# Level, state and convolution updates of VectorE in an earlier place, and two more unread products at the start

## The reference

```python
# block 1
mod = silu(c) @ ada_w + ada_b                     # 1024 x 6144, six vectors of 1024
h = rmsnorm(x, norm_mix_w) * (1 + sc1) + sh1
proj = h @ w_in                                   # 1024 x 3624, split into eleven parts
o_a = hgrn2_mixer(...)    # decayed linear recurrence, 4 heads of 128
o_b = dsa_mixer(...)      # scores, 128 best keys of each query, softmax, 4 heads of 64
o_c = conv_module(...)    # gate, causal depthwise convolution of 31 taps, layer norm
x = x + g1 * (concat(o_a, o_b, o_c) @ w_out)
x = x + g2 * (square(relu(h2 @ mlp_w1)) @ mlp_w2) # 4096 hidden channels
# block 2, layer A: gMLP mixer with 2048 channels
# block 2, layer B: RG-LRU, 12 heads of 128
xc = conv_b + sum over k of conv_w[k] * xb[t - 3 + k]     # 4 taps
r, i = sigmoid(xc @ gate_a_w + b), sigmoid(xc @ gate_x_w + b)
h[t] = a[t] * h[t-1] + sqrt(1 - a[t]**2) * i[t] * xc[t]   # a from r
x = x + (h * silu(g)) @ w_out
```

## Time and profile before

| | |
|---|---|
| median of 3 runs | 1294.99 us (1294.63, 1294.99, 1299.47) |
| the profiled execution | 1300.01 us |
| its span, first to last instruction | 1298.4 us |
| TensorE busy | 1258.8 us, 97% of the span |
| VectorE busy | 850.4 us, 66% |
| ScalarE busy | 584.2 us, 45% |
| mean granted clock of TensorE | 0.989 |

### The profile page before, as it was taken

One profiled execution on the slowest core, in us unless ns is written; L12 is line 12 of the kernel. 1 busy time (PEld: TensorE's weight loads), 2 busy tenths in 40 slices (PEclk: granted clock), 3 DMA queues, 4 the chain that ended last, 5 costly groups with the idle time before them and its releaser, 6 DMA issues.

```text
span 1298.4 us, 18826 instructions
## 1 busy us (share of the span) xinstructions
PE 1258.8 (97%) x6611; PEld 1024.2 (79%) x6611; DVE 850.4 (66%) x1275; ACT 584.2 (45%) x840; POOL 108.0 (8%) x149
## 2 busy tenths in 40 slices
PE   4999999999999999999999999999999999999997
PEld 3777778688788888888888888888888887777786
DVE  5889987648675322444444887775476668977863
ACT  4575545432354211333332665333233347878732
POOL 9124210000000000000000000110010000000000
PEclk9899999989999999999999999999999999999999
DMA  9677852315536333333332223324232241332131
GB/s 344 181 204 155 180 124 82 114 49 169 172 115 191 99 97 97 94 98 99 96 93 87 82 65 98 98 88 123 82 93 85 82 122 57 100 107 78 56 97 65
DMA packets 209084, 146.63 MB, mean 113 GB/s; under 512 B 7490, under 2 KB 191985, under 8 KB 209024
## 3 DMA queue, kind: packets, MB, share of 16 engines
q1 hardware_dynamic: 200672, 134.40, 34.4%
q0 software_dynamic: 6128, 10.38, 4.4%
q10 hardware_dynamic: 2224, 1.05, 0.3%
HBM read 135.06 MB, written 2.10 MB: 106 GB/s over the span
## 4 chain that ended last, share of the span: by engine, by line
PE 75%; DVE 13%; ACT 5%; issue 5%; DMA 2%; POOL 1%; DVEq 0%; ACTq 0%; POOLq 0%; SPq 0%
PE banks L404 23%; PE banks L406 22%; PE banks L405 22%; ACT w_hi L376 2%; DVE w_lo L388 1%; DVE xc L2438 1%; DMA cT<-in_c 1%; PE banks L708 1%; POOL e L2647 1%; DVE vh L2338 1%; DVE hgt L1900 1%; DVE acc_sh L1805 1%; DMA hq<-in_ada_w 1%; PE banks L1143 1%; PE banks L1088 1%
## 5 line engine op out<-in xcount | busy, mean ns | idle before, releaser
L388 DVE TENSOR_TENSOR w_lo<-raw,w_hi 128x1024 fp32r<-128x1024 f32 x204 | 250.8, 1234 | 127.2 <-ACT w_hi L376 122.2
L404 PE MATMUL banks<-h_hi,w_hi 128*128 128x512 f32 x792 | 319.8, 404 | 1.1 <-issue 0.5
L406 PE MATMUL banks<-h_hi,w_lo 128*128 128x512 f32 x792 | 310.4, 392 | 0.0
L405 PE MATMUL banks<-h_lo,w_hi 128*128 128x512 f32 x792 | 310.4, 392 | 0.0
L376 ACT ACTIVATE w_hi<-raw 128x1024 fp32r<-128x1024 f32 x204 | 213.4, 1051 | 156.2 <-PE banks L406 137.6
L404 PEld LDWEIGHTS banks<-h_hi,w_hi 128*128 128x128 f32 x792 | 150.1, 190 | 41.1 <-issue 9.2
L405 PEld LDWEIGHTS banks<-h_lo,w_hi 128*128 128x128 f32 x792 | 150.2, 190 | 33.7 <-issue 3.8
L406 PEld LDWEIGHTS banks<-h_hi,w_lo 128*128 128x128 f32 x792 | 149.9, 189 | 32.0
L404 PE MATMUL banks<-n_hi,w_hi 128*128 128x512 f32 x288 | 113.5, 394 | 0.9 <-DVE e L2400 0.9
L406 PE MATMUL banks<-n_hi,w_lo 128*128 128x512 f32 x288 | 112.1, 389 | 0.0
L405 PE MATMUL banks<-n_lo,w_hi 128*128 128x512 f32 x288 | 112.1, 389 | 0.0
(11 more groups left out here) (398 smaller groups left out, 1864.4 us busy)
## 6 DMA issues: line engine op xcount, KB each, us to landing
raw<-in_mlp_w SPq DMA_DIRECT2D x64, 512.0 KB, 3.8
raw<-in_a_w_in SPq DMA_DIRECT2D x48, 512.0 KB, 3.8
raw<-in_w_in SPq DMA_DIRECT2D x28, 512.0 KB, 4.2
raw<-in_ada_w SPq DMA_DIRECT2D x26, 512.0 KB, 4.2
raw<-in_b_w_in SPq DMA_DIRECT2D x24, 512.0 KB, 3.7
raw<-in_a_w_out SPq DMA_DIRECT2D x16, 512.0 KB, 3.4
raw<-in_b_w_out SPq DMA_DIRECT2D x16, 384.0 KB, 3.0
raw<-in_w_out SPq DMA_DIRECT2D x8, 512.0 KB, 4.0
```

Source lines behind the costliest of these rows:

```text
L388: dve.tensor_tensor(dst, src, hi, ALU.subtract).then_inc(split_lo, 1)
L404: pe.matmul(dst, l_hi, r_hi, start=first, stop=False)
L405: pe.matmul(dst, l_hi, r_lo, start=False, stop=False)
L406: return pe.matmul(dst, l_lo, r_hi, start=False, stop=last)
```

## The change

TensorE waits at the start after two more tiles (14 and 15) and runs `keep_busy()` after each, seven products for five. On VectorE, `level(6)` runs ahead of `lo_unit(25)` instead of behind it. `state(1)` stands at the end of slot 26 instead of in the middle of slot 27, and `state(2)` at the end of slot 27 instead of in slot 28. In the RG-LRU layer `conv(1, 2)` stands in turn 1 ahead of `recurrence(1, 1)`, with `lo_unit` of unit 12 in front of it, instead of at the start of turn 2; for that turn 2 is written out, and the loop is left with turns 3 and 4. ScalarE, GpSimd and SyncE keep their order.

```diff
-            for n in range(KT + 1, 2 * KT - 2):
+            for n in range(KT + 1, 2 * KT):
                 pe.wait_ge(ada_dve, n)
                 keep_busy()
...
             def slot(u):
 
+                level_first = u == U_LEVEL + 7
+                if level_first:
+                    level(u - U_LEVEL - 1)
                 lo_unit(dve, u + LEAD)
...
-                if U_LEVEL < u <= U_LEVEL + N_LEVELS:
+                if U_LEVEL < u <= U_LEVEL + N_LEVELS and not level_first:
                     level(u - U_LEVEL - 1)
...
                 if u == U_ATT + 4:
                     gate(1)
-                    state(1)
                     conv_scaled()
                 if u == U_ATT + 5:
                     gate(2)
                     softmax_in(3)
-                    state(2)
...
                 if u == U_ATT + 3:
                     softmax_out(2)
+                    state(1)
+                if u == U_ATT + 4:
+                    state(2)
...
-                if not first and more != "second":
+                if not first and more not in ("second", "third"):
                     conv(1, i)
...
                 recurrence(0, i)
-                if more is True and not first:
+                if more and more != "second" and not first:
                     conv(0, i + 1)
-                if first:
+                if first or more == "second":
                     lo_unit(dve, U_B + 5 + LEAD, i)
+                if more == "second":
+                    conv(1, i + 1)
                 recurrence(1, i)
-                if more and not first:
+                if more and more != "second" and not first:
                     lo_unit(dve, U_B + 5 + LEAD, i)
...
             turn(1, False, "second")
-            with dve.Fori(2, B_HEADS // 2 - 1) as i:
+            turn(2, False, "third")
+            with dve.Fori(3, B_HEADS // 2 - 1) as i:
                 turn(i, False, True)
```

## The result

The changed kernel takes 1288.91 us on the median of 8 runs (1286.99 to 1290.83), the kernel before 1297.12 us on the median of 8 beside it (1294.48 to 1301.30). The medians lie 8.2 us apart, 0.6%. The recorded ratio of the runs, which isn't the quotient of these two medians, is 0.9928, 95% interval 0.9911 to 0.9945: 0.7% faster. The profiled execution took 1288.7 us with a span of 1287.1, so 11.3 us of span are gone against the profile of before.

What follows compares the result with a forecast made beforehand. TensorE, busy 1258.8 of 1298.4 us, was taken as the bound, so only its pauses and half clock could be won. Terms 1.6 + 4.8 + 3.2 + 0.3 gave 9.9 us, 8.7 for the median: 1286 us, range 1281.5 to 1291.5.

Steps and rivals of the forecast that it cites:

- my sum: Gains of slot 22, states, conv and start added: 9.9 us for the profiled execution, 8.7 us for the median's.
- my signs of being right: No wait at three places, full clock behind, new pauses of about 1.6 and 1.0 us, `turn_probs(3)` 7 to 8 us sooner.
- my signs of being wrong: Half clock at 202 to 206 us, column sums after 34.7 us, pause above 2 us before turn 3, unexplained VectorE wait.
- Slot 22: `level(6)` moved ahead: 2.4 us gained with a new 1.6 us pause, 1.6 us after half a possible fall.
- States: `state(1)` and `state(2)` earlier in slots 26 to 28: 4.8 us gained, 2.8 without the clock's fall, 3.8 for the median.
- The conv of turn 2: `conv(1, 2)` earlier in the RG-LRU layer: 3.2 us gained, 1.8 without the fall, new pause of 1.0 us.
- The start: Two more products ahead of the column sums: net gain 0.3 us, bounds -1.9 and 2.9.
- push the column sums back by some 0.2 us: At the start, two more products delay the column sums by some 0.2 us, up to 1.9 at half clock.
- Rival 1: At all places, clock plays no part and only pauses are won: 7.0 us, 1288.0 us; chance 0.10.
- Rival 2: At slot 22, start and turn 3, new pauses replace the old: 2.5 us gained, 1292.5 us; chance 0.17.
- rival 3: Across the places, more falls go than counted: 12.9 us gained, 1282.1 us; chance 0.10.
- 4: Rival 4: turn 2's new straight code on VectorE waits for instructions, up to 15.7 us, giving 1302 us; chance 0.03.

Runs made afterwards that it cites:

- the first experiment: The kernel before with only the two more unread products at the start: 1296.93 us on the median of 12 runs, ratio 0.9985.
- the second profile of before: The kernel before, unchanged, profiled once more: one execution of 1296.08 us.
- the seventh: The changed kernel with `join(1)` right behind `level(6)` in slot 22: 1289.32 us on the median of 6, ratio 0.9928.
- the eighth experiment: The changed kernel with `yb_high(1, 1)` behind `read_gates(1, 2)` and `yb_low(1, 1)` behind VectorE's second input product: 1287.37 us, ratio 0.9910.
- the last two kernels: The changed kernel with `join(1)` forward, `yb_high(1, 1)` later and column sums halved: 1286.62 us with seven products at the start, 1284.68 us with five.

## Why the prediction was right

Predicted were 1286.0 us, 9.0 us below the median of before as it then stood, which is 0.7%; measured was 0.7% by the ratio and 8.2 us by the medians, for the 8.7 of my sum. The time itself came out 2.9 us higher. Most of that is the reference: beside the changed kernel, and in 59 later runs, the kernel before took 1293.96 to 1302.43 us with medians of 1297.1, 1299.2, 1299.0 and 1300.0, and the three runs of 1294.99 us were good ones. That the median's executions are some 5 us shorter than the profiled one was wrong: the profiled 1300.01 us lies 0 to 3 us above these four medians.

For the profiled execution I had 9.9 us, to 1290.1; it came out at 1288.7. The parts of the change gave 9.6 of them, and 1.7 us are the clock at the column sums, which is in no term of my sum. That the parts come so near to 9.9 is in part luck: the start was some 1 us worse than forecast and slot 22 0.7 us better.

Of my signs of being right, the missing waits, the full clock and both new pauses were seen. `turn_probs(3)` came 6.6 us sooner and not 7 to 8. Of my signs of being wrong one was seen: the column sums started at 36.41 us, later than 34.7.

**Slot 22.** Predicted 2.4 us with a new pause of 1.6 us ahead of `conv_mean`, and half a fall (0.8) taken off; measured 2.31 us, a pause of 1.42, and no fall in any of the five profiles that have it behind the moved level. That the half clock of level 7 had cost nothing is shown by the first experiment, for a fall as long as in the first profile; in the second profile of before it lasted longer and cost 2.1 us behind `conv_mean`, which my sum didn't foresee. That the join was late only by its place is shown by the seventh.

**States.** Predicted 4.8 us with the fall and 2.8 without; measured 5.0 and 3.3. `turn_probs(3)` was forecast 4.8 us sooner by this part and was 5.0.

**The conv of turn 2.** Predicted 3.2 and 1.8 us; measured 3.1 and 1.65 us (28.41 against 26.76). The new pause of 1.0 us was 1.23, and its cause, ScalarE's queue with `yb_high` in it, is shown by the eighth experiment. (My "four gate products" are the four records of two products; the 1.4 us are right.)

**The start.** Predicted was a gain of 0.3 us with bounds of -1.9 and 2.9; the profile shows a loss of 0.75 us up to level 6. The step that was mis-sized is "push the column sums back by some 0.2 us": they were 1.9 us late, its bad bound. The clock was at half from 25.8 to 32.6 us for 26.7 to 30.1 before; that delayed the first of the seven products by 0.95 us and stretched the first three. The half clock of 37.2 to 43.4 us did go, which gave back 1.0 us up to record 19 of the first units. In five of the six profiles with seven products the first product stood at 39.5 to 39.7 us; in the sixth, where the half clock at the start lasted 3.4 us for 6.8, at 37.9. With five products it stood at 37.8 to 38.1 in seven of eight, and at 38.6 in one. Level 6 started at 191.8 to 192.6 us with seven and at 190.6 to 192.2 with five; a part of that spread isn't from the start, since behind record 19 at 43.8 to 43.9 us it stood at 190.6, 191.2, 191.7 and 191.8. Yet the runs with the products alone were 2.3 us faster on the median, with a mean clock of 0.994 over 12 runs against 0.991 for 35 of before. Why is open: with the rest of the change it doesn't show (0.9928 against 0.9933), and in the last two kernels five products were no worse than seven.

**The clock.** What I treated as given, a fall behind each pause of 1.9 us or more, is not: of five profiles with the pause of `state(1)` that was not filled (two of before, and three of single parts) only one has the fall. Behind the pauses of `level(6)` and `conv(1, 2)` it fell in two of six profiles each. That the pauses have a part in it all the same is shown by the profiles in which they are gone: taken together, the clock fell at these three places in 5 of 17 cases with the pause, and in none of the 24 without it. Behind the shorter pauses of 1.2 to 1.5 us at line 744 and before turn 3 it never fell (14 cases). Nor is there a half clock anywhere else between 44 and 275 or between 290 and 1279 us in any of the 14 profiles.

So the gain of one execution is the pauses, 2.3 + 3.3 + 1.65 = 7.3 us, less some 0.7 for the start, and 1.5 to 2.1 us for each fall that would have come. With the shares seen in the profiles (one in five at 1.7 us, two in six at 1.5, one in six at 2.1) the falls are worth 1.2 us on average, an estimate: 7.8 us in all, where 8.2 were measured between the medians. The clock varies in the changed kernel too (0.993 to 0.995 over its 8 runs). Rival 1, that the clock plays no part, has its sum nearly right (7.0 us) and its reason wrong: a fall costs time when it comes, and it came only where a pause was left. Rival 2 was right about the direction at the start and about nothing else. Neither rival 3 nor 4 was seen: no wait of VectorE in turn 2 is left without a reason.

The Trainium skill, "TensorE: Matmul & The Clock Gate", section "HAM oscillation — how this bites in real kernels", warns only of longer idle gaps than these. The traces disagree in part: the clock fell behind a pause of 2.24 us in both profiles of the same kernel, and in none of four profiles of other kernels with a pause of 2.2 us at the same place. The same page's section "What's actually happening" says that the moment at which the clock changes is not tied to the kernel and shifts from run to run; the traces agree, since of two profiles of one kernel the first has falls behind all three pauses and the second behind one.

## What to carry to other kernels

A pause of the busiest engine is worth its length only if what stands behind it isn't late too: ask at once what is next, as `conv_mean` was for the join, and put that forward in the same move. When work is pushed back, follow it through the queue of the engine that reads it: with `yb_high` (and `yb_low`) where they stood, 1.4 us were lost with nothing to gain from their being early. And one profile isn't the kernel: before a fall of the clock goes into a sum, look at a second profile of the same program.

## What the runs showed of the hardware

- The clock's fall behind a pause is a matter of the execution. The same pause of 1.9 us was followed by 1.2 GHz once in five profiles, those of 2.2 and 2.8 us in two of six each, and it never fell at these places where the pause was gone (24 cases). The execution times of one unchanged program spread from 1293.96 to 1302.43 us. At a mean clock of 0.993 or 0.994 it took 1294.0 to 1298.3 us, and at 0.987 to 0.989 1300.1 to 1302.4; one of the 59 runs lists 0.942 at an ordinary 1299.22 us.
- Column sums (products with one moving column, each with a weight load) count as busy in the profile, yet the clock falls in a piece of 3.6 us of them or up to 1.2 us behind it: in ten of eleven profiles, for 3.4 or 6.8 us. Cut in two pieces with 2 us of full products between, it stayed up in three of three.
